# Two output banks by turns for the last layer's one-segment tiles, and squares summed on VectorE ahead of the statistics product

## The reference

```python
for l in range(DEPTH):                       # DEPTH = 2
    hx = rms_norm(x, norm_g[l, 0]) * (1.0 + sc1) + sh1
    hc = rms_norm(ctx, norm_g[l, 0]) * (1.0 + csc1) + csh1
    y_x, y_c = token_mixing(hx, hc, w_in[l], ...)      # y_c only in layer 0
    x = x + gate1 * rms_norm(y_x, norm_g[l, 1])
    hx = rms_norm(x, norm_g[l, 2]) * (1.0 + sc2) + sh2
    x = x + gate2 * rms_norm(swiglu(hx, w_ffn_in[l], w_ffn_out[l]), norm_g[l, 3])
    ...                                      # the same for ctx, in layer 0 alone
# token_mixing: one projection w_in feeds a short convolution, two RWKV scans, a
# neighbourhood attention and the gates; merge_branches: sum(sigmoid(gates) * proj) @ w_o
# rms_norm(y): y * rsqrt(mean(y * y, over 1024 channels) + EPS)
```

## Time and profile before

| | |
|---|---|
| median of 3 runs | 3738.24 us |
| profiled execution, its own time | 3747.26 us |
| its span | 3745.5 us |
| mean granted TensorE clock | 0.969 of full speed |
| TensorE matmul busy | 3455.7 us (92%) |
| VectorE, ScalarE, GpSimd busy | 1558.5, 1201.6, 825.8 us |
| layer 0's output stage | about 1401 to 1479 us in the span |
| last layer: prologue, bodies and tail, attention | about 2145 to 2243, 2243 to 2959, 2959 to 3187 us |
| last layer's output stage | about 3281 to 3332 us |

### The profile page before, as it was taken

The page is one execution under the profiler, slowest core; times in us unless marked ns, Lnnn a source line. Parts: engine busy times, 40 slices in busy tenths (PEclk is TensorE's granted clock), DMA queues, the critical chain, the costliest instruction groups (busy, mean ns, idle before and its releaser), DMA issues.

```text
span 3745.5 us, 79837 instructions
## 1 busy us (share of the span) xinstructions
PE 3455.7 (92%) x34184; PEld 2708.3 (72%) x34184; DVE 1558.5 (42%) x2970; ACT 1201.6 (32%) x2588; POOL 825.8 (22%) x520
## 2 busy tenths in 40 slices
PE   6999999999899898899999789999999888789998
PEld 4777777777677787788888467676766666658886
DVE  3445454544454561200144444645554455530023
ACT  4333333332333333311112433333333333342222
POOL 1211111101122132222333121111111132324453
PEclk8999999999999999999999889999999999899999
DMA  4423333333344341121211141413132232523322
GB/s 185 125 95 103 114 106 109 97 116 128 107 148 154 127 155 47 49 62 62 62 56 62 67 111 59 114 50 114 58 108 92 76 103 73 180 64 95 95 90 78
DMA packets 246704, 364.93 MB, mean 97 GB/s; under 512 B 154096, under 2 KB 155376, under 8 KB 245888
## 3 DMA queue, kind: packets, MB, share of 16 engines
q1 hardware_dynamic: 226976, 294.57, 25.8%
q10 hardware_dynamic: 14976, 35.66, 2.5%
q0 software_dynamic: 4448, 30.24, 2.3%
HBM read 291.20 MB, written 69.21 MB: 96 GB/s over the span
## 4 chain that ended last, share of the span: by engine, by line
PE 78%; DVE 6%; issue 4%; ACT 4%; DVEq 2%; DMA 2%; PEld 1%; POOLq 1%; POOL 1%; ACTq 0%; SPq 0%; PEldq 0%
PE banks L279 20%; PE banks L280 17%; PE banks L281 17%; PE banks L935 3%; PE banks L1543 3%; PE banks L1530 2%; PE banks L1539 2%; PE banks L1887 2%; PE banks L1500 1%; PE banks L502 1%; PE banks L386 1%; PE banks L1552 1%; DVE arena L587 1%; DMA slot<-in_w_mix 1%; PE banks L1870 1%
## 5 line engine op out<-in xcount | busy, mean ns | idle before, releaser
L279 PE MATMUL banks<-hx_rounded,branch_weights_high 128*128 128x512 f32 (+1 forms) x1352 | 539.7, 399 | 75.1 <-DVE resid_rounded L536 20.6
L281 PE MATMUL banks<-hx_rounded,slot_rounded 128*128 128x512 f32 (+1 forms) x1664 | 589.8, 354 | 0.0
L279 PE MATMUL banks<-hx_high,weight_parts 128*128 128x512 f32 (+1 forms) x1560 | 555.8, 356 | 19.4 <-DVE hx_low L536 18.9
L848 POOL TENSOR_TENSOR slot_rounded<-slot,branch_weights_high 128x512 fp32r<-128x512 f32 x188 | 242.0, 1308 | 1479.5 <-ACT branch_weights_high L843 1478.2
L280 PE MATMUL banks<-hx_low,weight_parts 128*128 128x512 f32 (+1 forms) x1560 | 555.1, 356 | 0.0
L281 PE MATMUL banks<-hx_high,weight_parts 128*128 128x512 f32 (+1 forms) x1560 | 553.3, 355 | 0.0
L280 PE MATMUL banks<-resid_rounded,branch_weights_high 128*128 128x512 f32 (+1 forms) x1352 | 478.4, 354 | 0.0
L279 PEld LDWEIGHTS banks<-hx_rounded,branch_weights_high 128*128 128x128 f32 x1352 | 261.8, 194 | 160.9 <-issue 100.9
L281 PEld LDWEIGHTS banks<-hx_rounded,slot_rounded 128*128 128x128 f32 x1664 | 322.2, 194 | 44.7
L279 PEld LDWEIGHTS banks<-hx_high,weight_parts 128*128 128x128 f32 x1560 | 295.8, 190 | 68.0 <-issue 22.6
L281 PEld LDWEIGHTS banks<-hx_high,weight_parts 128*128 128x128 f32 x1560 | 295.5, 189 | 42.4
(11 more groups left out here) (238 smaller groups left out, 6114.3 us busy)
## 6 DMA issues: line engine op xcount, KB each, us to landing
slot<-in_w_mix SPq DMA_DIRECT2D x120, 512.0 KB, 3.8
slot<-in_w_ffn_in SPq DMA_DIRECT2D x88, 512.0 KB, 3.5
arena<-chunk_inputs SPq DMA_DIRECT2D x48, 640.0 KB, 4.1
arena<-in_w_ada SPq DMA_DIRECT2D x50, 512.0 KB, 4.1
slot<-in_w_ffn_out SPq DMA_DIRECT2D x44, 512.0 KB, 3.5
slot<-in_w_ada SPq DMA_DIRECT2D x40, 512.0 KB, 3.8
chunk_inputs<-arena SPq DMA_DIRECT2D x80, 256.0 KB, 3.3
arena<-side_projections POOLq DMA_DIRECT2D x16, 1152.0 KB, 6.3
```

What stands on the lines that cost most here:

```text
L279: first = nc.tensor.matmul(out, w_hi, x_hi, start=start, stop=False)
L281: return first, nc.tensor.matmul(out, w_lo, x_hi, start=False, stop=stop)
L848: last = nc.gpsimd.tensor_tensor(slots_r[g % 3][:, half], slots[g % 3][:, half], weights_high(g)[:, half], ALU.subtract)
```

## The change

Two edits, and one that only renames. First, in the last layer a tile with one segment goes to bank 7 and bank 6 by turns: `tile_bank` counts the one-segment tiles ahead of it, tile 3 has bank 7, tile 4 bank 6, and so on. Two-segment tiles and the small products stay where they were. Second, the output stage takes no statistics behind each tile: VectorE adds the squares of tiles 0 to 6 into a buffer (6 additions, in the space of a merge gate), and TensorE takes the statistics at the end, once for the sum and once for the square of tile 7. Third, the 8 semaphores for the input tiles' loads and the 8 for the residual tiles' stores are one set of 8, with the threshold 32 in place of 16 where the second use is waited for.

```diff
+        def tile_bank(l, g, s):
+
+            if len(tile_segs(l, g)) == 2:
+                return s
+            return 1 - sum(len(tile_segs(l, y)) == 1 for y in range(g)) % 2
+
+        def tile_out(l, g, s):
+            return bank[6 + tile_bank(l, g, s)][:, 0:SEGS[s][1] - SEGS[s][0]]
...
-                        banks_of.free(s)
-                    first, last = hx_product(pair(6)[s], weights_high(g), slots_r[slot], k, s)
+                        banks_of.free(tile_bank(l, g, s))
+                    first, last = hx_product(tile_out(l, g, s), weights_high(g), slots_r[slot], k, s)
...
-                        banks_of.busy[s] = (seg_taken[s], seg_count(l, g, s))
+                        banks_of.busy[tile_bank(l, g, s)] = (seg_taken[s], seg_count(l, g, s))
...
-                        nc.scalar.activation(dst, pair(6)[s], ACT.Copy).then_inc(seg_taken[s], 1)
+                        nc.scalar.activation(dst, tile_out(l, g, s), ACT.Copy).then_inc(seg_taken[s], 1)
...
+        SQ_SUM = GATE[0][:, 0, :]
+        sq_summed = Count(sem("squares_summed"))
+
+        def out_dve(dve, l):
+            use, lo = 4 * l + 1, SEGS[segs_of(l)[0]][0]
+            for m in range(1, KD - 1):
+                dve.wait_ge(sq_made.sem, sq_made.ready(use, m))
+                last = nc.vector.tensor_tensor(SQ_SUM[:, lo:T], NSQ[0][:, lo:T] if m == 1 else SQ_SUM[:, lo:T], NSQ[m % 2][:, lo:T], ALU.add)
+                last.then_inc(sq_used.sem, 2 if m == 1 else 1)
+                dve.drain()
+            dve.drain().then_inc(sq_summed.sem, 1)
...
-                if m:
-                    stats_pe(pe, use, segs, [m - 1])
-            stats_pe(pe, use, segs, [KD - 1])
+            for source, made in ((SQ_SUM, sq_summed), (NSQ[(KD - 1) % 2], sq_made)):
+                pe.wait_ge(made.sem, made.ready(use if made is sq_made else l, KD - 1 if made is sq_made else 0))
+                for s in segs:
+                    last = nc.tensor.matmul(stats_bank(use)[s], MEAN_D, source[:, SEGS[s][0]:SEGS[s][1]], start=made is sq_summed, stop=made is sq_made)
+            last.then_inc(sq_used.sem, 1)
...
                 merge_dve(dve, l)
+                out_dve(dve, l)
                 add_dve(dve, 2 * l, 0, segs_of(l), Y)
```

More of the change, by code:

```diff
@@ L202, in program @@
         ada_full = [sem(f"ada_slab_loaded_{j}") for j in range(2 * KD)]
-        x_loaded = [sem(f"input_tile_loaded_{k}") for k in range(KD)]
+        tile_moved = [sem(f"residual_tile_{k}_moved") for k in range(KD)]
         ada_moved = Count(sem("ada_rows_in_sbuf"), 4)
@@ L213, in program @@
         lora_high = sem("lora_weights_rounded")
-        resid_kept = [sem(f"residual_tile_{k}_in_dram") for k in range(KD)]
         resid_back = sem("residual_loaded_again")
@@ L444, in opening_act @@
             for k in range(KD):
-                act.wait_ge(x_loaded[k], 16)
+                act.wait_ge(tile_moved[k], 16)
                 square(act, 0, k, RES[:, k, :], NSQ[k % 2]).then_inc(sq_made.sem, 1)
@@ L533, in rest_dve @@
             if use == 2:
-                dve.wait_ge(resid_kept[k], 16)
+                dve.wait_ge(tile_moved[k], 32)
             high, rest = of_norm(half)
@@ L1938, in eviction @@
                         act.wait_ge(seg_prod[s], seg_count(l, g, s))
-                        nc.scalar.activation(SPILL_ATT[b][:, SEGS[s][0]:SEGS[s][1]], pair(6)[s], ACT.Copy).then_inc(seg_taken[s], 1)
+                        nc.scalar.activation(SPILL_ATT[b][:, SEGS[s][0]:SEGS[s][1]], tile_out(l, g, s), ACT.Copy).then_inc(seg_taken[s], 1)
                     yield at((g, segs[-1])) + 1
@@ L2569, in _ @@
             for k in range(KD):
-                act.dma_start(RES[:, k, :], a["x"][:, k * T:(k + 1) * T]).then_inc(x_loaded[k], 16)
+                act.dma_start(RES[:, k, :], a["x"][:, k * T:(k + 1) * T]).then_inc(tile_moved[k], 16)
             opening_act(act)
```

2 lines of the change are left out of this document (1 added, 1 removed).

## The result

The changed kernel takes 3726.46 us (median of 7 runs, 3719.67 to 3733.10), the kernel before on the same chip 3739.24 us (median of 7). The ratio is 0.9961, with a 95% interval of 0.9948 to 0.9975: 14.6 us faster, between 9.3 and 19.4. The forecast was 24.6 us faster, 3713.5 us, with a range that ended at 3723. The direction was right, the time lies 3.5 us outside the range, and 10.0 us of the forecast 24.6 are missing. The same kernel in a second session, five timed executions more, had a ratio of 0.9959 (0.9946 to 0.9972).

What follows compares the result with a forecast made beforehand. TensorE, busy 92% of the span, was taken as the bound. Terms 12.8 + 0.3 + 0.7 + 3.6 + 7.2 = 24.6 us off 3738.24 gave 3713.6, forecast as 3713.5 us; own range 3709 to 3718, wider range 3704 to 3723.

Steps and rivals of the forecast that it cites:

- The statistics, 12.8 us: Output stages: six fewer statistics products each, saving 7.6 us in layer 0 and 5.2 us in the last layer.
- The additions, 0 us: Output stages: VectorE's six additions of squares cost nothing; bounds 0 to 0.1 us a tile in the last layer.
- Prologue, bodies, tail, 1.0 us: Bank alternation there saves 0.3 us in the prologue and 0.7 us in bodies and tail.
- the 0.96 us: Each body: tile 6 in bank 6 starts 0.96 us later behind the key norm's second read; taken as 0.
- Attention, 10.8 us: Last layer's attention: bank alternation saves 3.6 us at the first head pair and 7.2 us at other waits.
- The meeting with GpSimd: First head pair: VectorE's additions fall on GpSimd's subtraction and lose 1.2 to 2.4 us, leaving 3.6 us gain.
- the 2.2 us that the sum has for tile 50: Attention: part of the 7.2 us for other waits; tile 50 waited 2.00 us for ScalarE's copy.
- Rival 1: Attention gives back less and bodies pay 2.9 us: gain 15.9 us, 3722 us; chance 0.16.
- Rivals 2, 3 and 4: 2: claim not given, chance 0.15. 3: bank 6 waits, slower, 3744, 0.03. 4: GpSimd's low weights bind, 3718, 0.06.
- What I take off is taken off the median.: Whole kernel: savings summed on the profiled execution (3747.26 us) are subtracted from the runs' median, 3738.24 us.

Runs made afterwards that it cites:

- sums_only: Kernel before with only the squares summed on VectorE and statistics products at the end of each output stage, banks as before; ratio 0.9978, 10.3 us less.
- banks_bodies: Kernel before with banks 7 and 6 alternating only for one-segment tiles of prologue, bodies and tail; ratio 1.0011, 4.2 us more.
- banks_flipped: Changed kernel with the two banks exchanged in the alternation (tile 3 in bank 6, tile 4 in bank 7); ratio to the kernel before 0.9963, 14.0 us less.
- after_busy: Changed kernel plus unread constant products keeping TensorE busy ahead of its waits in four places; ratio to the kernel before 0.9953, 17.7 us less.
- banks_only: Kernel before with only the alternation of banks 7 and 6, statistics as before; ratio 0.9974, 10.0 us less.
- banks_attention: Kernel before with the bank alternation for attention's 16 tiles alone; ratio 0.9979, 7.5 us less.
- stats_doubled: Kernel before with each statistics product of the output stages issued twice; ratio 1.0056, 22.3 us longer.
- shift_8: Kernel before plus 8 unread constant products ahead of output tile 4 in layer 0, where TensorE never idles; ratio 1.0021, 8.3 us more.
- the 114: 114 timed executions of the unchanged kernel before, from five sessions on four chips, without the first comparison's seven; mean 3742.9 us.
- shift_4: Kernel before plus 4 unread constant products ahead of output tile 4 in layer 0; ratio 1.0009, 4.9 us more.
- shift_15: Kernel before plus 15 unread constant products ahead of output tile 4 in layer 0; ratio 1.0025, 8.9 us more.
- best: Changed kernel with alternation in attention alone and half a tile's products per head pair moved behind the permutation; ratio to the kernel before 0.9935, median 3717.37 us.
- best_shift_2: Changed kernel with attention-only alternation, earlier permutation and 2 added constant products in layer 0's output stage; ratio to the kernel before 0.9940, 24.2 us less.
- before_busy: Kernel before plus unread constant products keeping TensorE busy ahead of its waits in four places; ratio 1.0027, 10.5 us more.

## Why the prediction was wrong

**The statistics, 12.8 us: right.** Periods of 8.34 and 5.44 us were measured against 8.35 and 5.44 forecast. Over all profiles layer 0's stage takes 73.80 us with eight statistics and 66.08 with two (6 and 8 profiles, alike to 0.04 us). sums_only gave 10.3 us.

**The additions, 0 us: right**, and they hide between two subtractions.

**Prologue, bodies, tail, 1.0 us: right in the waits** (0.34 us later where the second reader is waited for, 1.0 us at tile 7, the 0.96 us for the most part under the wait behind it, which fell by 0.64). In time they were not: banks_bodies was 4.2 us slower, and the stretch was 2.8 us longer in the mean of six profiles.

**Attention, 10.8 us: right.** The stretch took 227.2 us in the mean of nine profiles without the alternation there and 215.6 in seven with it, 11.5 us less (0.6). Of these 24.0 and 19.2 us were at the lower clock, so up to 2.4 us of the 11.5 are clock, of which the forecast had counted about 1.5 at the first head pair. The meeting with GpSimd cost 1.76 us where 1.2 to 2.4 were foretold. (The place of the meeting was worked out 0.2 us off: 5.4 us sooner than 2975.76 is 2970.3 and not 2970.1, which changes nothing.) No run shows by itself the 2.2 us that the sum has for tile 50: measured are its 2.00 us of idle time before and none after, with its first product at 3028.26, 0.23 us behind the product in front. Rival 1, that attention gives back less, did not come about, though its 3722 us is the nearest number on the list. Rivals 2, 3 and 4 did not either.

**The step that failed** is the sentence "What I take off is taken off the median." It takes for granted that the rest of the program runs as it did, and so puts the clock of all other stages at nothing, without a reason. It does not run so: the part of the time that TensorE spends at the lower clock differs from kernel to kernel, with mean clocks from 0.9674 (banks_flipped) to 0.9724 (after_busy). In the changed kernel the mean clock was 0.9692 instead of 0.9709, and the stretch from prologue to tail, where the forecast took 1.0 us off, grew (844.9 and 848.6 us against 844.6 and 844.1). Within the executions of one kernel, the time falls by 2.28 us (0.12) for each 0.001 of mean granted clock (260 executions of 18 kernels, each against its own mean). Brought to the clock of before by that slope, the kernels stand so:

| kernel | forecast by the terms | measured | at the clock of before |
|---|---|---|---|
| changed kernel | -24.6 | -17.8 (1.4) | -21.5 (0.7) |
| sums_only | -12.8 | -10.3 (1.2) | -12.7 (0.7) |
| banks_only | -11.8 | -10.0 (1.4) | -11.3 (0.6) |
| banks_attention | -10.8 | -7.5 (1.4) | -9.5 (0.9) |
| banks_bodies | -1.0 | +4.2 (1.2) | -0.1 (0.8) |
| stats_doubled | +17.1 | +22.3 (1.7) | +18.8 (1.4) |
| shift_8 | +1.8 | +8.3 (1.5) | +3.8 (0.6) |

The last column is worked out and not measured, but it shows the size: of the 6.8 us missing in the mean, 3.7 go with the clock. The other 3.1 us have no proven cause. Against the first comparison, where 10.0 us are missing, 3 us more come from the seven executions of before, whose mean lay 3 us below that of the 114. That a lower clock goes with a longer time is measured; how much of the missing time it causes rests on the slope. The sum was also made from one profile of before, of an untypically long execution. Its attention took 227.65 us, and the second profile's 224.91, but over nine profiles the mean is near the first, so that cost the attention term nothing.

**What stays open.** Shown is that the clock falls in nearly every kernel that is not the one before, also in those that only delay (shift_4, shift_8, shift_15) or add (stats_doubled), so that it is not a price of the edits at their places. Not shown is why before stands at 0.9709 and the others at 0.9674 to 0.9704. That the stages of before happen to lie well would fit, but nothing here tests it. A shift by 3.3 us did not bring it back. best and best_shift_2 have before's clock (0.9708, 0.9712), six executions each.

**The range.** 3704 to 3723 was built from the unknown prices of waits alone. Single executions of one kernel spread over 14 us (before: 3733.4 to 3747.4 in one session of 27) and a pure delay of 1.8 us moved the mean by 8. A term of 0 to 7 us for the clock belongs in the range, and would have held the result; its size is known only from these runs.

## What to carry to other kernels

A sum of terms from one profile can be right in each of them and still miss the timed difference, because the unchanged code around the edit may not get the same clock: here a delay of 1.8 us ahead of it (shift_8) came with 8.3 us more, and with 55.9 us at the lower clock in the stretch from prologue to attention, where before had 48.2 and 52.3. Below half a per cent, forecast the terms and the clock apart, and judge an edit by the mean clock of its executions beside their time. And a wait that goes can leave its time to the next in line: here 11.6 us of waits for copies made those for the rotation 4.1 us longer, and moving work against those brought up 9.5 us, behind a rounding that waited for its weights. Read what is queued in front of the releaser before moving more.

## What the runs showed of the hardware

- The granted clock of TensorE is recorded at full speed or at 0.5 of it. In the first profile of before 18 of the 40 stretches at 0.5 lasted 3.4 us, 17 6.8 us and 4 10.2 us.
- A product of 128 x 128 in fp32 took 0.22 us of TensorE at the full clock, and 0.43 us at 0.5 of it (before_busy).
- A delay of 1.8 us in fully busy TensorE work, with nothing else changed (shift_8), made a kernel of 3743 us 8.3 us longer (1.5), and the mean granted clock fell from 0.9709 to 0.9689.
- Products that only keep TensorE busy ahead of its waits raised the mean clock (to 0.9719 from 0.9709 in before, to 0.9724 from 0.9692 in the changed kernel) and did not make the kernel faster (10.5 us longer, and 17.7 us below before where it was 17.8).
- Six kernels with the code of before in the stretch from the last layer's prologue to its tail took 2 to 7 us longer there (846.1 to 851.3 us against 844.6 and 844.1).
- Two additions of 64 x 512 on VectorE took 4.05 us instead of 2.29 beside GpSimd's subtraction in two halves, which itself took 3.28 us instead of 2.51. The four instructions ended by turns, about 1.0 us apart.
- Two profiles of one kernel differ by 7.5 us of span (3745.5 and 3738.0), with the same waits in the bodies to 0.4 us for each pair of lines.
